# Hybrid mLSTM / sparse-attention / expert block on one core: the layout of the experts' down weights

## The reference

```python
def run_block(args):              # one block of at most 128 rows of one expert
    toks, gts, ei = args
    xb = hf[toks]                                     # rows x 1024
    hb = jax.nn.silu(xb @ w1[ei]) * (xb @ w3[ei])     # 1024 x 512 each
    return (hb @ w2[ei]) * gts[:, None]               # 512 x 1024
```

## Time and profile before

| | |
|---|---|
| runs of the kernel | 1533.39, 1536.89, 1537.32 us; median 1536.89 |
| the profiled execution's own time | 1532.91 us |
| span of the instructions in it | 1531.0 us |
| PE busy | 1347.4 us, 88% of the span |
| DVE, ACT, POOL busy | 601.9, 396.8, 82.0 us |
| moved by DMA | 327.22 MB |
| issues of expert weights | 99, 2048 KB each |
| mean granted TensorE clock | 0.945 of full speed |

### The profile page before, as it was taken

How to read it: one execution, slowest core, us unless ns; L and a number is a source line. 1 busy time by engine, 2 the same in 40 slices (tenths; PEclk the granted TensorE clock), 3 DMA queues, 4 the chain that set the end, 5 groups by cost and what they waited for, 6 DMA issues and landing times.

```text
span 1531.0 us, 17228 instructions
## 1 busy us (share of the span) xinstructions
PE 1347.4 (88%) x6333; PEld 678.0 (44%) x6333; DVE 601.9 (39%) x1339; ACT 396.8 (26%) x878; POOL 82.0 (5%) x113
## 2 busy tenths in 40 slices
PE   4999999999996889988899964999999899999950
PEld 3644444464664445444455532444434343444320
DVE  3526446410344766666522255222322222222216
ACT  4234211113666555555222210000000000000005
POOL 0000000010003000000000000000000000000014
PEclk9899999999997999999999975999999999999985
DMA  9713145220004880000352272999999999999969
GB/s 339 163 42 104 63 163 199 76 111 0 1 1 115 233 276 1 1 1 1 134 237 97 83 274 86 380 389 405 395 405 403 402 401 414 402 413 393 417 231 300
DMA packets 109980, 327.22 MB, mean 214 GB/s; under 512 B 26812, under 2 KB 51528, under 8 KB 101320
## 3 DMA queue, kind: packets, MB, share of 16 engines
q1 hardware_dynamic: 96824, 296.19, 51.7%
q0 software_dynamic: 6288, 18.90, 3.9%
q10 hardware_dynamic: 6784, 11.02, 1.9%
HBM read 285.69 MB, written 43.02 MB: 215 GB/s over the span
## 4 chain that ended last, share of the span: by engine, by line
PE 28%; SPq 16%; DMA 6%; DVE 4%; issue 3%; ACT 2%; POOL 1%; PEldq 1%; PEld 0%; DVEq 0%; ACTq 0%; POOLq 0%
SPq L660 14%; PE ps L1482 7%; PE ps L1524 5%; DMA arena<-expert_w 5%; PE ps L1535 3%; PE ps L1574 3%; PE ps L1383 2%; PE ps L1400 2%; PE ps L1420 2%; SPq L709 1%; SPq L658 1%; ACT arena L1049 1%; POOL arena L851 1%; PE ps L1462 1%; PE ps L1514 1%
## 5 line engine op out<-in xcount | busy, mean ns | idle before, releaser
L1236 PE MATMUL ps<-arena 128*128 128x512 f32 x512 | 222.0, 593 | 0.0
L1535 PE MATMUL ps<-arena 128*32 128x256 f32 (+1 forms) x1408 | 196.1, 494 | 22.0 <-DMA arena<-expert_w 19.7
L1574 PE MATMUL ps<-arena 128*32 128x256 f32 (+2 forms) x832 | 152.6, 498 | 1.8 <-DMA arena<-expert_w 1.8
L1236 PEld LDWEIGHTS ps<-arena 128*128 128x128 f32 x512 | 96.6, 190 | 117.8 <-issue 117.7
L1247 PE MATMUL ps<-arena 128*128 128x512 f32 (+1 forms) x384 | 145.2, 537 | 1.4 <-DVE arena L1670 1.4
L1535 PEld LDWEIGHTS ps<-arena 128*32 128x32 f32 (+1 forms) x1408 | 74.1, 125 | 130.1 <-issue 112.0
L1524 PE MATMUL ps<-arena 128*128 128x512 f32 x256 | 114.7, 605 | 2.8 <-DVE arena L2106 2.8
L1482 PE MATMUL ps<-arena 128*128 128x512 f32 x256 | 112.7, 592 | 0.1
L1049 ACT ACTIVATE arena<-arena 128x640 f32<-128x640 f32 (+7 forms) x128 | 92.7, 726 | 59.5 <-DVE arena L1883 59.5
L1247 PEld LDWEIGHTS ps<-arena 128*128 128x128 f32 x384 | 73.3, 193 | 66.5 <-issue 58.8
L1111 ACT ACTIVATE arena<-ps 64x512 f32<-64x512 f32 x20 | 11.8, 589 | 336.6 <-PE ps L1535 336.6
(11 more groups left out here) (345 smaller groups left out, 1283.8 us busy)
## 6 DMA issues: line engine op xcount, KB each, us to landing
arena<-expert_w SPq DMA_DIRECT2D x99, 2048.0 KB, 34.5
arena<-ada_w SPq DMA_DIRECT2D x12, 2048.0 KB, 9.1
d_y<-arena SPq DMA_DIRECT2D x25, 512.0 KB, 6.5
arena<-x SPq DMA_DIRECT2D x16, 512.0 KB, 4.2
arena<-w_in SPq DMA_DIRECT2D x4, 2048.0 KB, 10.8
d_y<-arena ACTq DMA_DIRECT2D x40, 128.0 KB
arena<-w_out SPq DMA_DIRECT2D x2, 2048.0 KB, 8.5
out<-arena SPq DMA_DIRECT2D x8, 512.0 KB, 3.0
```

Source lines behind the costliest of these rows:

```text
L1236: last = nc.tensor.matmul(b, w(k), hT[:, k, 512 * c:512 * c + 512], start=(k == 0), stop=(k == KT - 1))
L1535: last = nc.tensor.matmul(ps[width * j:width * j + width, 2 if width == 64 else 3, 0:span], xgT[s][:, k, lo:lo + width], w_up[slots[n]][:, ...
L1574: last = nc.tensor.matmul(dst, hid_T[s][:, at_:at_ + width], w_down[slot][:, k, span * j:span * j + span], start=(k == 0), stop=(k == 3))
```

## The change

Three lines. The down weights are read with rows 4p to 4p+3 on partition p, one piece of 16 KB per partition. The k-th product of the down stage then needs the middle values 4p+k on partition p. For parts of 64 and 128 rows the transposes take every fourth middle value (`k::4`) in place of 128 neighbours. For parts of 32 rows the two transposes stay as they are; instead the four up products there read their weights in another order, every fourth column of the weight row, 128 of them from column b and then 128 from column b+1 (b = 0 for the first half and 2 for the second), so that the middle values are put out in the order that is wanted. Numbers, sizes and order of the instructions on every engine, and the DMAs, are the same as before; only access patterns differ.

```diff
@@ load_weight
                 if n == 2:
-                    sp.dma_start(w_down[j], src.rearrange("a (k p) n -> p (a k) n", p=P)).then_inc(w_in[j], 16)
+                    sp.dma_start(w_down[j], src.rearrange("a (p k) n -> p (a k) n", p=P)).then_inc(w_in[j], 16)
@@ f_up, parts of 64 and 32 rows
                             n, at_ = span * j // 512, span * j % 512
+                            w = w_up[slots[n]][:, k, :]
+                            if width == 32:
+                                w = w.rearrange("p (a b) -> p b a", b=4)[:, at_ // P:at_ // P + 2, :]
                             last = nc.tensor.matmul(ps[width * j:width * j + width, 2 if width == 64 else 3, 0:span],
-                                                    xgT[s][:, k, lo:lo + width], w_up[slots[n]][:, k, at_:at_ + span],
+                                                    xgT[s][:, k, lo:lo + width], w,
                                                     start=(k == 0), stop=(k == KT - 1))
@@ f_turn_hidden
-                        last = nc.tensor.transpose(ps[:, 4 + s, wide * k:wide * k + wide], hid_e[s][0:wide, P * k:P * k + P],
+                        last = nc.tensor.transpose(ps[:, 4 + s, wide * k:wide * k + wide], hid_e[s][0:wide, k::4],
                                                    ident[0:wide, 0:wide])
```

## The result

The changed kernel takes 1552.93 us (median of 4 runs, 1552.15 to 1555.20) against 1536.30 us for the kernel before (4 runs, 1533.39 to 1537.32): a ratio of 1.0114, 95% interval 1.0096 to 1.0132. It is slower by 16.6 us, by over the 0.3% that can be told. The profiled execution has a span of 1550.9 us, 19.9 more than before; the one before was the fastest of its four runs.

What follows compares the result with a forecast made beforehand. DMA was taken to lead stage F, with PE nearly level. PE work of 46.5 + 4 us less 33.7 us to spare gave 16.8 us; 1536.9 + 17 = 1554 us, 8-in-10 range 1524 to 1568, own range 1545 to 1568.

Steps and rivals of the forecast that it cites:

- The bound now: In expert stage F, DMA was said to lead, with a share of 1.01 at 402 GB/s from 1100 to 1475 us.
- The slack of 33.7 us: In stage F, PE could get 33.7 us more work before setting the end: 21.5 us waits plus 12.2 us low clock.
- The strided up products, 46.5 us: In stage F's 32-row up products, stride 4 reads add 3.87 us per part, 46.5 us of PE work over 12.
- The strided transposes, 4 us of a possible 6.9: In the 112 middle-value transposes, strided loads take 62 ns more each: at most 6.9 us of PE work, 4 taken.
- The gain of the pieces, 0 to 12 us, 8 taken: Over 30 down loads in stage F, 16 KB pieces save DMA 0 to 12 us, 8 taken, hidden if PE leads.
- rival 1: In the 32-row up products, stride 4 streams at full speed and DMA leads, faster: 1527 us, 1525 to 1532; chance 0.27.
- The sum: Stage F: PE work grows 50.5 us against 33.7 us to spare, so PE leads and the kernel is 16.8 us slower.
- 1.8 to 2 times the stream's time: The forecast's own case for the strided 32-row up products: 1545 to 1568 us, chance 0.50.
- the third rival: 32-row up products cost 1.8 to 2.9 us more per part, DMA's gain and PE's growth cancel: 1537 us; chance 0.10.
- Stride 4 at full speed: Same as rival 1: stride 4 in the 32-row up products costs no streaming time; 1527 us, chance 0.27.
- Streams that disturb each other: Four side-by-side 32-row up-product streams take turns: 1643 us, milder about + 60; chance 0.13 for anything above + 32 us.

Runs made afterwards that it cites:

- the pieces alone: The kernel before with only the down weights read in one piece of 16 KB per partition: 1530.68 us, ratio 0.9975.

## Why the prediction was right

**The bound now.** "DMA leads" holds: the pieces alone, which change nothing on PE, gave 4 us, and 26 us more PE work in the 96-row steps gave none.

**The slack of 33.7 us.** Waits of 21.5 us and 12.2 us of low clock. Both are gone after: no wait for weights, and (631 - 595) x 640 / 2 = 11.5 us from the clock, 33.0 us in all. The size was right. That it is one stock, which my sum took for granted, isn't: in the kernel with stride in the five steps of 32 rows, 8 of 19 us were paid though PE still waited 16.1 us elsewhere, by its trace for work right at the start, where it holds back the slots, and at the end, where hardly a wait is left to take it from. It made no difference to the sum here, since the whole slack was used up anyway and PE led from end to end.

**The strided up products, 46.5 us.** A part went up by 3.77 us by the timeline above; 12 of them make 45.2 us. The row I took it from (one stream in stride 8 over the whole array) carried over to four streams side by side in stride 4 with 1.80 against 1.82 ns. Taking them out gave back 22 to 23 us: the 17 that the slack had not covered, and 5 because DMA leads again and the gain of the pieces is seen.

**The strided transposes, 4 us of a possible 6.9.** Measured 4.8 us in stage F where PE leads, nothing that is seen where DMA does.

**The gain of the pieces, 0 to 12 us, 8 taken.** This term was mis-sized: alone it is 4 us (2 to 6). The row it was taken from, 8.6 against 8.2 us of shortest time to landing, doesn't show the pieces at all: with down loads in one piece their shortest time is 8.7 us in the kernel with the pieces alone and 9.0 in the changed one, and that of the up loads 8.1. Where the 4 us come from is open (last section). Since the gain is hidden behind PE in the changed kernel (1554.25 us without it, 1552.93 with it), the error didn't reach the forecast. It would have mattered for rival 1: its 1527 had such a gain in it, and the kernel with contiguous up products, which is nearest to it, took 1530.

**The sum.** 46.5 + 4 - 33.7 = 16.8 us; measured 16.6 us between the medians, but 19.8 between the two profiled executions (1532.91 and 1552.74 us), and the sum was made on the profiled one: 1549.7 was expected of it, 3 us too few. With the measured terms it is 45.2 + 4.8 - 33.0 = 17.0 us. The rest isn't accounted for. That the forecast of 1554 lies within 1.1 us is partly luck: the profiled execution before was 3.4 us under its median, the one after 0.2.

**The labels of two rivals.** "1.8 to 2 times the stream's time" doesn't fit the numbers beside it: my own price, 466 against 224 ns, is 2.08 times, the range 1545 to 1568 goes by the same sum with 1.9 to 2.4 times, and measured were 2.05. And the third rival's 1.8 to 2.9 us per part would be no change only from about 2.1 us on; below that the sum gives a gain.

**The rivals.** Stride 4 at full speed fell with the 32-row group at 633 ns (I had 623). Streams that disturb each other fell too: four at 1.80 ns for a column, one at 1.82. The Trainium skill (Advanced Engine Details and Errata, SBUF Cachelines) asks for at least two hits on a line of 16 bytes. This case agrees: in stride 2, with two columns to a line, a part costs 3.83 us, 7% over the 3.59 of the contiguous one, in stride 3, with four columns to three lines, 5.66 us, and in stride 4 7.36 us.

## What to carry to other kernels

Before a layout is changed for a DMA's sake, ask who reads it and how: a moving operand of TensorE whose neighbours lie 16 bytes or more apart took about twice the time here. For an operand that is loaded into the array, each load took about half as long again (213 against 140 ns), and the 112 of them cost 4.8 us. Where two engines are nearly level, work out the slack of the one that follows from its waits and from the low clock behind them, and see how much of it lies where it can be used: work at the start, where it holds back the leader's buffers, and work around the leader's last delivery were paid here in part, about 5 of 15 us at the start and 2.7 of 3.8 at the end. And put an awkward order where it is cheap: turning the small middle values cost PE 16 short instructions per part, 1.1 us in place of 0.3, reading the big weights out of order 3.8 us.

## What the runs showed of the hardware that I had not expected

A streamed float32 operand was priced here by how often it steps into another 16 bytes, at 1.80 to 1.87 ns each time in the strides measured (2, 3, 4 and 8), as long as the steps add up to more than the columns' own 0.87 ns each. Four streams side by side (1.80 ns in stride 4, 1.83 in stride 8) paid no more than one (1.82).

SyncE's time at issue fell with the number of pieces. The issues of expert loads by line, kernel before first, then the changed one, duration in ns (min/median/max):

```profile
L660 SPq DMA_DIRECT2D arena<-expert_w x66: 337/927/15313, 752.9 to 1432.4; - x66
```

```profile
L660 SPq DMA_DIRECT2D arena<-expert_w x66: 337/338/780, 753.2 to 1441.5; - x66
```

With 16 KB pieces in all loads an issue never took over 0.8 us there, nor over 1.1 us in the pieces-alone kernel, where DMA is as full as before; with two pieces of 8 KB the longest was 8.1 us, with four 15.3 (7.7 in the changed kernel with four pieces, where PE leads). I read the stretches of SyncE's queue in the chain of before as a queue full of pieces, not a cause of their own: without them an up load waited longer behind the others instead (median 39.7 us from issue to landing in the pieces-alone kernel, 33.9 before), and only 4 us came of it. What fills up isn't shown by a run. Why it is 4 us and not 0 or 12, that is, whether the pieces move faster or the stream has fewer gaps, stays open; the windows at 402 GB/s don't resolve it.
